# Input-projection tiles in pairs by one level of Strassen's scheme, in a two-layer diffusion backbone

## The reference

```python
h = _rmsnorm(x, norm_g) * (1.0 + scale) + shift
z = h @ w_in                                   # 1024 -> 9472 columns
hy_z, hy_g, rw_z, rw_g, da_q, da_k, da_v, da_g, mg = split(z)
y_a = hyena(hy_z, hy_g)                        # centred conv of 3, long convolution by FFT, gate
y_b = rwkv(rw_z, rw_g)                         # two scans, forward and backward, summed, group norm, gate
y_c = diff_attention(da_q, da_k, da_v, da_g)   # QK norm, rotary, two softmax maps, gate
merged = sum(sigmoid(mg_b) * (y_b @ w_br[b]))  # three branches
x = x + gate * (merged @ w_out)
```

## Time and profile before

| | us |
|---|---|
| median of 3 runs | 2820.41 (2816.99 to 2828.57) |
| span of the profiled execution (the page gives no other time for it) | 2826.2 |
| PE busy | 2653.4 (94%) |
| DVE, ACT, POOL busy | 1166.5, 623.9, 160.3 |
| mean granted clock of PE | 0.976 of full speed |

### The profile page before, as it was taken

The page is one execution under the profiler, slowest core; times in us unless marked ns, Lnnn a source line. Parts: engine busy times, 40 slices in busy tenths (PEclk is TensorE's granted clock), DMA queues, the critical chain, the costliest instruction groups (busy, mean ns, idle before and its releaser), DMA issues.

```text
span 2826.2 us, 58242 instructions
## 1 busy us (share of the span) xinstructions
PE 2653.4 (94%) x26080; PEld 1665.9 (59%) x26080; DVE 1166.5 (41%) x1938; ACT 623.9 (22%) x1182; POOL 160.3 (6%) x197
## 2 busy tenths in 40 slices
PE   6999997899999999999999999979999989899999
PEld 3546674466666666555545556645667666665555
DVE  2552726653636363110143537256545554522111
ACT  3111115332323231000021111243323232310000
POOL 0010000010101010000000100000101010100000
PEclk9999999999999999999999999989999999999999
DMA  6111130100000000121441111301000101012212
GB/s 260 51 43 60 46 115 12 38 26 25 26 25 26 25 26 25 60 97 60 150 141 44 49 60 57 108 1 46 19 32 19 34 18 32 19 34 66 97 60 67
DMA packets 40208, 155.13 MB, mean 55 GB/s; under 512 B 4992, under 2 KB 4992, under 8 KB 38944
## 3 DMA queue, kind: packets, MB, share of 16 engines
q1 hardware_dynamic: 35856, 131.09, 14.2%
q0 software_dynamic: 4112, 20.39, 2.0%
HBM read 144.64 MB, written 6.82 MB: 54 GB/s over the span
## 4 chain that ended last, share of the span: by engine, by line
PE 87%; DVE 7%; ACT 2%; issue 2%; DMA 1%; POOL 0%; DVEq 0%; PEld 0%; SPq 0%; ACTq 0%; POOLq 0%
PE ps L556 85%; DVE scr L1852 1%; DVE scr L1874 1%; PE ps L1008 1%; PE ps L842 1%; DVE scr L1997 1%; DMA ring<-in_w 1%; DVE scr L1864 0%; DVE scr L1865 0%; ACT scr L1580 0%; DMA cst<-in_cst 0%; PE ps L980 0%; DVE scr L1676 0%; DVE scr L1985 0%; ACT scr L1320 0%
## 5 line engine op out<-in xcount | busy, mean ns | idle before, releaser
L556 PE MATMUL ps<-h,ring 128*128 128x512 f32 (+1 forms) x4480 | 1264.6, 439 | 15.9 <-ACT h L1311 11.3
L556 PEld LDWEIGHTS ps<-h,ring 128*128 128x128 f32 x4480 | 695.2, 192 | 576.2 <-issue 570.5
L556 PE MATMUL ps<-scr 32*32 32x32 f32 (+9 forms) x17704 | 664.7, 226 | 66.3 <-issue 23.7
L556 PEld LDWEIGHTS ps<-scr 32*32 32x32 f32 (+5 forms) x17704 | 512.5, 122 | 220.6 <-issue 164.0
L2095 DVE SCALAR_TENSOR_TENSOR scr<-scr,ps 128x640 f32<-128x640 f32 x32 | 26.3, 821 | 325.6 <-PE ps L556 325.2
L556 PE MATMUL ps<-scr,ring 128*128 128x512 f32 (+1 forms) x512 | 141.9, 438 | 4.0 <-DVEq L2100 4.0
L556 PE MATMUL ps<-scr,cst 64*64 64x128 f32 (+2 forms) x544 | 115.9, 372 | 9.4 <-ACT scr L1515 9.4
L1604 ACT ACTIVATE scr<-ps 128x640 f32<-128x640 f32 x32 | 22.5, 703 | 434.9 <-PE ps L556 434.9
L556 PEld LDWEIGHTS ps<-scr,ring 128*128 128x128 f32 x512 | 78.6, 192 | 67.0 <-issue 62.6
L2013 DVE COPY_PREDICATED scr<-cst,ps 128x80 f32<-128x80 int32 x128 | 32.2, 251 | 173.8 <-PE ps L556 173.5
L1804 DVE RECIPROCAL scr<-scr 128x640 f32<-128x640 f32 x16 | 66.4, 4153 | 73.6 <-ACT scr L1373 73.6
(11 more groups left out here) (260 smaller groups left out, 2223.8 us busy)
## 6 DMA issues: line engine op xcount, KB each, us to landing
ring<-in_w SPq DMA_DIRECT2D x240, 512.0 KB, 3.5
x<-in_x SPq DMA_DIRECT2D x1, 2560.0 KB, 16.2
yc<-in_win POOLq DMA_DIRECT2D x2, 1280.0 KB, 9.2
x<-in_x POOLq DMA_DIRECT2D x1, 2560.0 KB, 10.6
out_y<-x POOLq DMA_DIRECT2D x8, 320.0 KB, 6.5
x<-out_y POOLq DMA_DIRECT2D x1, 2560.0 KB, 9.5
out_y<-x SPq DMA_DIRECT2D x8, 320.0 KB, 3.2
scr<-in_inv POOLq DMA_DIRECT2D x2, 1152.0 KB, 5.5
```

The source lines that it names most:

```text
L556: return nc.tensor.matmul(out, lhsT, rhs, start=start, stop=stop)
```

## The change

Every two projection tiles of a pair are made by seven products of half the inner dimension (four k-steps), one tile of features and half the tokens (320 columns, HALF), in Winograd's form, where eight quarters would be needed. With A the weights (A11, A12 the halves of the first tile, A21, A22 of the second) and B the halves of h, the sums on the weight side are made by POOL per pair (S1 = A21 + A22, S2 = S1 - A11, A11 - A21, A12 - S2; 512 columns each), those on the side of h once per layer by DVE (16 subtractions of 320 columns, T1 to T4, partly in x). The products add onto three PSUM banks; ACT copies four partial results to SBUF and DVE adds three others onto them. z is from then on read in SBUF. The early gates are four pairs, in 28 pieces of one k-step over both directions; they are spilled to memory, and read back before their use. Other edits: Sqrt and reciprocal of all norms but the first become Ln and Exp on ACT; av is made like the others and transposed by PE; the GATE slots come in fours behind a pair of ag tiles; the scan tiles are ordered rk, rv, rr, rg, with the small products at other places; x comes back in two halves.

```diff
-for _j in range(JT):
-    ORDER += [("z", f"ag{_j}")] + GATE[2 * _j:2 * _j + 2]
+for _j in range(0, JT, 2):
+    ORDER += [("z", f"ag{_j}"), ("z", f"ag{_j + 1}")] + GATE[2 * _j:2 * _j + 4]
...
+FIRST_PAIR_ORDER = {1: 1, 2: 2, 5: 3, 6: 4, 7: 5}
+PAIR_ORDER = {1: 1, 5: 2, 6: 3, 2: 4, 7: 5}
...
+            return {"a": n % 2, "b": 1 - n % 2, "c": 2}[role]
...
+                def sums_of(n):
...
+                    nc.gpsimd.tensor_tensor(S1, b[:, 0:512], b[:, 512:1024], ALU.add).then_inc(summed, 1)
+                    pool.wait_ge(summed, 4 * n + 1)
...
+                    nc.gpsimd.tensor_tensor(S2, S1, a[:, 0:512], ALU.subtract).then_inc(summed, 1)
+                    nc.gpsimd.tensor_tensor(b[:, 0:512], a[:, 0:512], b[:, 0:512], ALU.subtract).then_inc(summed, 1)
+                def last_sum_of(n):
...
+                    pool.wait_ge(z_prod, product_count(n, 1))
+                    pool.wait_ge(summed, 4 * n + 3)
+                    nc.gpsimd.tensor_tensor(a[:, 0:512], a[:, 512:1024], S2, ALU.subtract).then_inc(summed, 1)
...
+                def product6(n):
+                    pe.wait_ge(summed, 4 * n + 2)
+                    pe.wait_ge(z_copied, 4 * n + 1)
+                    for k in range(4):
+                        if n == 0:
+                            pe.wait_ge(t_ready, 9 + k)
+                        i = mm_more(half_bank(bank_of("a", n)), S2[:, k * 128:(k + 1) * 128], T2(k), k == 3)
+                    i.then_inc(z_prod, 1)
...
+                def product7(n):
+                    w = weights("z", PAIRS[n][1])
+                    pe.wait_ge(summed, 4 * n + 3)
+                    pe.wait_ge(z_copied, 4 * n + 3)
+                    run("a", n, w[:, 0:512], T3).then_inc(z_prod, 1)
...
+                def product4(n):
+                    w = weights("z", PAIRS[n][1])
+                    if n == 0:
+                        pe.wait_ge(t_ready, 16)
+                    pe.wait_ge(z_added, 3 * n + 2)
+                    run("a", n, w[:, 512:1024], T4).then_inc(w_used, 1)
...
+                product1(0, marks=True)
+                product2(0)
+                product5(0)
+                product6(0)
+                last_three(0)
...
+                for i in range(2):
+                    n = PAIR_AV + 1 + i
+                    first_four(n)
+                    turn_v(2 * i)
+                    turn_v(2 * i + 1)
+                    last_three(n)
+                pe.wait_ge(v_done, JT)
+                for q in range(4):
+                    rows_of_mod(4, q, weights("gate", 0, q))
+                first_four(PAIR_AG + 1)
...
+                    n = PAIR_R + 2 * j
+                    product1(n)
+                    product5(n)
                     if j >= 1:
                         norm_sums(j - 1)
+                    product6(n)
+                    product2(n)
                     if j >= 1:
                         norm_squares(j - 1)
+                    product7(n)
...
+                    low_rank(j, 0)
+                    product3(n)
+                    product4(n)
+                    n += 1
+                    product1(n)
+                    product5(n)
+                    product6(n)
                     pe.wait_ge(kk_sq, j + 1)
+                    pe.wait_ge(th_ready, 2 * j + 1)
                     wide_mm(4, bones, kksq).then_inc(kk_ss, 1)
+                    product2(n)
...
+                    product7(n)
+                    pe.wait_ge(root_read, 2 * JT + HEADS + 2 * j + 1)
+                    pe.wait_ge(vT_ready, j + 1)
+                    low_rank(j, 1)
+                    product3(n)
+                    product4(n)
+                    pe.wait_ge(th_ready, 2 * j + 2)
...
+                        parts = ((0, 2), (2, 4), (4, 6), (6, 10), (10, 12), (12, 16)) if d == 0 else (
+                            (16, 18), (18, 20), (20, 21), (21, 24), (24, 25), (25, 28))
...
+                def inverse_roots(*norms):
...
+                        A_(dst, src, ACT.Ln, scale=scale, bias=eps(e)).then_inc(root_read, 1)
...
+                        i = A_(dst, dst, ACT.Exp, scale=-0.5)
...
+                head_roots(0)
                 lin("wl", tw, dcol("ommu", 12), 0.0)
...
+                head_roots(1)
                 lin("al", tal, dcol("ommu", 13), 0.0)
...
+                def added(n, p):
...
+                    TTn(z[:, cols], half_bank(bank_of(bank, n)), z[:, cols], ADD).then_inc(z_added, 1)
...
+                dve.wait_ge(x_saved, l * (16 * KD))
+                dve.wait_ge(xn_ready, KD)
+                for k in range(4):
+                    dve.wait_ge(h_ready, k + 5)
+                    TTn(T3(k), B22(k), T1(k), SUB).then_inc(t_ready, 1)
+                    dve.wait_ge(t_ready, 2 * k + 1)
+                    TTn(T1(k), T1(k), B11(k), SUB).then_inc(t_ready, 1)
+                dve.wait_ge(t_ready, 8)
+                for k in range(4):
+                    TTn(T2(k), B22(k), T1(k), SUB).then_inc(t_ready, 1)
+                dve.wait_ge(t_ready, 12)
+                for k in range(4):
+                    TTn(T4(k), B21(k), T2(k), SUB).then_inc(t_ready, 1)
                 do(TS(dcol("hmu", 0, 14), pcol("mu", 0, 14), 0.5, None, MUL))
...
                 for j in range(JT):
+                    n = PAIR_R + 2 * j
+                    if j >= 1:
+                        centred(j - 1)
+                    all_added(n)
+                    if j >= 1:
+                        normed_heads(j - 1)
                     taps(f"rk{j}", k_, dcol("hmu", 4 + j), dcol("hmu", 4 + j))
                     dve.sem_inc(k_ready, 1)
...
```

817 lines of the change are left out of this document (554 added, 263 removed).

## The result

The changed kernel takes 2793.8 us (median of 4 runs, 2788.1 to 2799.9), the kernel before 2820.8 beside it: ratio 0.9898, 95% interval 0.9875 to 0.9921. It is faster by 1.0%, 27 us, where 76 were forecast. The profiled execution has a span of 2794.9. The interval of one ratio is 4 to 10 us either way, so two versions whose gains lie less than some 10 us apart are not told apart by their times.

A forecast was written before the change was run, and what follows sets the result against it. PE, busy 94% of the span, was taken to bound the kernel. Terms summed to -38.1 us per layer, -76.2 for two, from 2826.2; less 5.8 this gave 2744.2 us, with an 8-in-10 range of 2675 to 2808.

The forecast's parts named there:

- values: Value tiles made as two pairs plus 20 transposes, instead of four token-first tiles: -1.4 us per layer.
- The rival of the clock: Each new PE stand loses 3.1 us to the lower clock, eight more a layer, 50 in all: 2794; chance 0.15.
- The products: Projection pairs made by seven products cost 15.23 us instead of 17.41: -76.3 us per layer.
- Start of a layer: First pair: PE stands on an ACT copy behind the sine, then runs slower: +17.8 us per layer (6.5 to 25).
- End of the FFT: First gate pair's last product waits for DVE's addition queued behind spectrum products, POOL's sums delaying it: +8.7 us per layer.
- Ahead of each doubling: Before the doublings: PE waits removed, -14.9 us per layer; DVE's key chain becomes late, +13.2 (0 to 28).
- early pairs: Backward pieces filling PE while ACT and DVE work are shorter, keeping about 1.4 of 2.2: +3.2 us per layer.
- GpSimd: POOL's sums block DVE operations with two SBUF inputs: 5.0 us at FFT's end, 1.3 at start, 13.2 before doublings, per layer.
- The rival of GpSimd's sums on VectorE's chain: Ahead of the doublings every POOL sum delays PE: 15.2 us per stretch instead of 3.3, 2839 in all; chance 0.08.
- Roots: Sqrt becoming Ln and Exp on ACT delays PE: +4.6 us in lora stage, +2.0 in query stage, per layer.
- Gates: Four modulation slots in a row empty the weight ring; PE waits for loads: +5.0 us per layer (2 to 8).

The follow-up runs named there:

- the filler: Changed kernel plus 20 unused products in TensorE's first-pair stand and 8 ahead of the filter products: ratio 0.9890 to the kernel before.
- The run with the new order: Changed kernel with each forward doubling's head reordered: first-level blocks ahead of receptance's taps, products and gate, B's first products behind: ratio 0.9822 to the kernel before.
- the reorders: Changed kernel with layer start, Fourier-stage end and forward-doubling head reordered, and early pairs' GpSimd sums moved behind the taps: 2715.8 us, ratio 0.9621.

## Why the prediction was wrong

The direction and the range held; the gain was 27 us, not 76 (31 by the two spans, from which the forecast was made).

**The step that failed is the clock.** The prediction put time at the lower clock into its sum once a layer: 3.1 us at the start, 6.2 in all. It cost 42 us more than before. The other parts of the sum, each taken whole, were near: the products and values 154 us (155 forecast), PE's idle time 81 us more (73, which is what the terms make without the 3.1). Of the 45 us that are missing between the spans, 36 are the clock's and 8 idle time. The rival of the clock had it: it took 50 us more for it, and its time, 2794, is the measured one. The prediction held against it that most stands are under 5 us; but behind the stand of 3.93 us at the filters eight matmuls took 7.19 us for 3.70, and behind one of 3.85 us ahead of the key pair's sixth product (558.40) that product took 4.60. The rival's places were right in part: 18 us of the 42 lie at the two starts, 12 in the doublings, where it had 25. That the stands bring the lower clock was shown at the starts, by the filler; elsewhere it is argued from the runs in which stands and lower clock went together.

That the idle time came out so near is partly luck, as its places show. By the prediction's own steps:

- *The products*, -76.3 a layer: right. A pair starts 2.2 us sooner than two tiles did.
- *Start of a layer*, +17.8: mechanism right, size wrong by 9 us a layer, some 6 of them the clock's. The first stand came as foreseen (from 66 to 76.3; it was 67.6 to 79.0). What failed is that the count stopped at the end of the first pair. The same chain, additions, taps, arguments, sine, is late once more at the filter products: 3.93 us, with 5.7 lost at the half clock behind it. Without GpSimd's sums this stand was 0.41, so it is their collision with VectorE, for which the prediction had 1.3 here.
- *End of the FFT*, +8.7: about the right size (10.4 on average, the pair's own 2.2 counted) for the wrong reason. I put the wait on VectorE's addition. In the changed kernel it is ScalarE, whose third spectrum copies stand ahead of the pair's; VectorE's wait appeared only when that was mended.
- *Ahead of each doubling*, -14.9 and +13.2, with *early pairs*, +3.2: the place with the largest error, 15 us a layer, some 6 of them the clock's. The stretch from the first key product to the blocks is 6.7 us shorter, where two pairs and the waits removed make 8.1. From the blocks to the next j a pair of doublings takes 4.1 us more than before, where 3.3 of lateness less 1.4 kept by the early pieces made 1.9. Together 2.5 us are gained where 6.2 were forecast. The run with the new order shows what 2.8 of the 4.1 were; with it 1.4 are left. The chain from the first key to the gate was added up without asking in which order VectorE would serve PE: the first level, which PE needs at once, stood behind three steps (taps, product, gate) that it needs later.
- *GpSimd*, priced at 19.5 a layer in three places: 25 by the run without sums. The price at the Fourier stage (5.0) was too high (1.9), at the start (1.3) it was too low (8.8), and for the stretches (13.2) about right. The rival of GpSimd's sums on VectorE's chain had the mechanism, not the price: 3.8 a stretch, far from the 12.8 from which it was to decide.
- *The clock*: see above. The cost is an estimate of PE's busy time, and not all of it need be gained in the span: the filler run gave 6.2 and 8.5 us back at the starts, and the whole moved by 2 to 6.
- *Roots* were costed for ScalarE only (+4.6, +2.0: 3.85 and 2.0 measured). Taking out two reciprocals was given no term of its own; undone, it costs 63 us. That was not an error of the sum, since the chain had been counted without them, but the prediction did not say that the whole gain hangs on it.
- *Gates*, +5.0: 6.0 measured (waits of 0.52, 2.32, 0.94, 0.46 and 1.76 for the weight DMA in layer 0; 5.5 in layer 1).

About tables, the Trainium skill (ScalarE: Activation LUTs, "Table sets") says that ln and exp come in one set, so that the two need one load. The trace does not agree: the changed kernel loads a table 28 times at the line of the logarithm and 28 times at that of the exponential, 1.28 us each, 63 loads in all against 35. The prediction's bound with a load for each was the real case. It would have put 1.3 us more per pair on the query stage; the waits there were 0.5 per pair all the same, as forecast without that load, which no run explains and which is luck.

## What to carry to other kernels

When a scheme takes work from the busiest engine and gives sums to three others, price the order in which those others serve it, place by place and past the first late place: here the reorders alone are worth 78 us, three times what the change brought as it stood. Count behind each new stand of TensorE what the lower clock costs, and check busy time for it: here busy time fell by 112 us where the work had shrunk by 154. An engine with slack on average (VectorE 42%) can still be the one all wait for, and there a part that is worth nothing alone, like the roots, can carry the whole gain. Move a background engine's blocks of work away from the short operations of the critical one, and look again after each reorder, because the critical operations move too.

## What the runs showed of the hardware

- One GpSimd sum of 128x512 stretches a VectorE operation by some 1.0 us, whatever its own length: 0.34 to 1.36, 0.75 to 1.70, 0.82 to 1.90, 0.49 to 1.23. Short ones suffer most in proportion. GpSimd's own 1.26 becomes 1.7 to 1.8.
- A load of ScalarE's table takes 1.28 us and the next activation starts right behind it (loads at 718.54 and, in the kernel before with the new roots, 701.08; activations at 719.84 and 702.38). An Exp behind an Ln loads a table again.
- After the stands of 11.42 and 3.93 us TensorE's granted clock was 0.50 for the products that followed; with filler matmuls in the stand it stayed at 1.00 and the same products took 2.39 and 3.70 us for 4.01 and 7.19.
